# Layer-0 projection, output projection and scan: sums and transposes in two parts, transposes amid products, scan inputs in column pieces

## The reference

```
# layer 0: input projection and per-head work (gdn_sequence)
proj = h @ w_in                                   # q, k: 8 heads; v, z: 16 heads, 128 wide
qkv = silu(short_conv(qkv, conv_w))               # 4 taps along the tokens
q, k = l2norm(q), l2norm(k)                       # per token and head
...                                               # delta rule, both directions -> o_f, o_b
o = rmsnorm(o_f + flip(o_b), norm_g) * silu(z)
y = o.reshape(B, T, 2048) @ w_out                 # output projection of layer 0
# layer 1: gates and scan (rglru_sequence)
r = sigmoid(xblk @ w_r + b_r); i = sigmoid(xblk @ w_i + b_i)
log_a = -8 * r * softplus(-lam); a = exp(log_a)
b = sqrt(-expm1(2 * log_a)) * (i * xc)
h = scan of h[t] = a[t] * h[t-1] + b[t], once forwards, once backwards
```

## Time and profile before

| what | value |
|---|---|
| median of 3 runs | 4576.62 us (4575.06 to 4580.44) |
| profiled execution: its own time, and its span | 4570.06 us, 4568.1 us |
| TensorE busy | 4101.5 us (90%), 30756 matmuls |
| VectorE, ScalarE, GpSimd busy | 2332.6, 2279.5, 2017.4 us |
| mean granted clock of TensorE | 0.948 of full speed |
| costliest groups | L565 (products of the projection), three of 710 to 725 us |

### The profile page before, as it was taken

How to read it: one execution, slowest core, us unless ns; L and a number is a source line. 1 busy time by engine, 2 the same in 40 slices (tenths; PEclk the granted TensorE clock), 3 DMA queues, 4 the chain that set the end, 5 groups by cost and what they waited for, 6 DMA issues and landing times. The chain is left out here.

```text
span 4568.1 us, 83170 instructions
## 1 busy us (share of the span) xinstructions
PE 4101.5 (90%) x30756; PEld 3422.6 (75%) x30756; DVE 2332.6 (51%) x2947; ACT 2279.5 (50%) x4473; POOL 2017.4 (44%) x1524
## 2 busy tenths in 40 slices
PE   6689999999999969999999999986999599978779
PEld 2367777777777758888888888875888488856657
DVE  3234433444434446666666666655554423238853
ACT  4335555555654636666666666652111511148832
POOL 2245555555545546677777777743111412100022
PEclk8789999999999989999999999998999599988889
DMA  6245544445445456676667666654443322354245
GB/s 229 86 126 149 150 141 143 146 145 149 143 144 149 145 177 198 198 200 197 198 197 199 196 200 197 200 166 172 175 178 138 97 105 113 126 204 188 82 136 138
DMA packets 775798, 733.24 MB, mean 161 GB/s; under 512 B 111808, under 2 KB 702656, under 8 KB 758272
## 3 DMA queue, kind: packets, MB, share of 16 engines
q1 hardware_dynamic: 775456, 728.67, 51.3%
HBM read 483.12 MB, written 245.33 MB: 159 GB/s over the span
## 5 line engine op out<-in xcount | busy, mean ns | idle before, releaser
L565 PE MATMUL pj_bank<-h_hi,pj_whi 128*128 128x512 f32 (+1 forms) x1920 | 724.6, 377 | 21.0 <-POOL pj_wlo L551 20.8
L565 PE MATMUL pj_bank<-h_lo,pj_whi 128*128 128x512 f32 (+1 forms) x1920 | 711.7, 371 | 0.0
L565 PE MATMUL pj_bank<-h_hi,pj_wlo 128*128 128x512 f32 (+1 forms) x1920 | 710.0, 370 | 0.0
L751 POOL TENSOR_TENSOR pj_BD<-pj_E,pj_gi 128x512 f32<-128x512 f32 x144 | 194.6, 1352 | 650.4 <-ACT pj_E L888 650.4
L1354 ACT ACTIVATE dc_R<-dc_psE 128x256 f16<-128x256 f32 x864 | 285.0, 381 | 371.4 <-PE dc_psE L1231 371.3
L1428 DVE TENSOR_TENSOR dc_Y<-dc_psY,dc_pick 128x256 f16<-128x256 f32 x864 | 325.1, 417 | 277.7 <-PE dc_psY L1217 277.7
L565 PEld LDWEIGHTS pj_bank<-h_hi,pj_whi 128*128 128x128 f32 x1920 | 366.8, 191 | 88.9 <-POOL pj_wlo L551 21.3
L565 PEld LDWEIGHTS pj_bank<-h_lo,pj_whi 128*128 128x128 f32 x1920 | 365.9, 191 | 64.9 <-issue 5.7
L565 PEld LDWEIGHTS pj_bank<-h_hi,pj_wlo 128*128 128x128 f32 x1920 | 365.1, 190 | 62.0
L933 DVE RECIPROCAL pj_acc<-pj_acc 128x2304 f32<-128x2304 f32 x16 | 232.8, 14553 | 260.8 <-ACT pj_acc L865 260.8
L1146 POOL TENSOR_TENSOR dc_A<-dc_Lhi,dc_id 128x512 f16<-128x512 f16 x144 | 166.3, 1155 | 416.0 <-ACT dc_Lhi L1345 416.0
(11 more groups left out here) (267 smaller groups left out, 10394.3 us busy)
## 6 DMA issues: line engine op xcount, KB each, us to landing
dc_dd<-scratch_decays SPq DMA_DIRECT2D x288, 256.0 KB, 5.5
dc_tm<-scratch_tm SPq DMA_DIRECT2D x288, 192.0 KB, 2.5
pj_E<-scratch_cgrow SPq DMA_DIRECT2D x288, 128.0 KB, 3.7
scratch_decays<-pj_E SPq DMA_DIRECT2D x144, 256.0 KB, 3.8
scratch_decays<-pj_BD SPq DMA_DIRECT2D x144, 256.0 KB, 3.7
dc_fm<-scratch_fm SPq DMA_DIRECT2D x288, 128.0 KB, 3.3
dc_egr<-scratch_egrow SPq DMA_DIRECT2D x288, 128.0 KB, 3.7
scratch_o<-dc_ob SPq DMA_DIRECT2D x288, 128.0 KB, 3.1
```

Of the source, the lines that this page charges most:

```text
L565: i = pe.matmul(self.bank[blk][:, 0:n], l[b][:, k, :], r[:, k, at:at + n], start=(m == 0), stop=(m == 3 * KT - 1))
L751: pool.tensor_tensor(BD[b][:], E[b][:], gi[b][:, :, Q_BETA, :].unsqueeze(3).broadcast_to(C4), ALU.mult).then_inc(s["d_scaled"], 1)
```

## The change

**Projection of layer 0.** The sums and transposes are cut in two parts, pieces 0 to 2 and pieces 3 and 4 (`PARTS`). Part 0 stands after block 3, part 1 after block 4. The keys' transposes stand later by one block: part 0 after V0's block 4, part 1 after V1's block 0. ScalarE's reads are cut alike (`beside`). The store of the keys' transposes moves on SyncE's queue behind two `finish`.

```diff
+        PARTS = (range(3), range(3, NB))
@@ sync, stage
-                    if j == V1:
-                        store_tm(h, "trK", 0)
                     if j:
                         finish(h, j - 1, 2, last)
...
                     finish(h, j, 0, last)
+                    if j == V1:
+                        store_tm(h, "trK", 0)
@@ tensor, stage
                         pr.products(pe, h, j, blk, first)
-                        if blk != 3:
+                        if j == V0 and blk == NB - 1:
+                            turn(h, K, "trK", 0)
+                        if j == V1 and blk == 0:
+                            turn(h, K, "trK", 1)
+                        if blk < 3:
                             continue
                         if j == Q and not first:
-                            turn(h - 1, V1, "trV1")
+                            turn(h - 1, V1, "trV1", blk - 3)
                         if j == Z0:
-                            norms(h, Q)
+                            norms(h, Q, blk - 3)
                         if j == Z1:
-                            norms(h, K)
-                        if j == V0:
-                            turn(h, K, "trK")
+                            norms(h, K, blk - 3)
                         if j == V1:
-                            turn(h, V0, "trV0")
+                            turn(h, V0, "trV0", blk - 3)
@@ scalar
+                def beside(h, j, first, part):
+                    if j == Q and not first:
+                        collect(h - 1, V1, "trV1", part)
+                    if j == Z0:
+                        root(h, Q, part)
+                    if j == Z1:
+                        root(h, K, part)
+                    if j == V0 and part == 1:
+                        collect(h, K, "trK", 0)
+                    if j == V1:
+                        collect(h, V0, "trV0", part)
+
                 def stage(h, j, first):
                     decay(h, j, 0)
                     take(h, j, 0, first)
+                    if j == V1:
+                        collect(h, K, "trK", 1)
                     take(h, j, 1, first)
...
                     take(h, j, 2, first)
                     take(h, j, 3, first)
...
+                    beside(h, j, first, 0)
                     decay(h, j, 2)
                     take(h, j, 4, first)
+                    beside(h, j, first, 1)
```

```diff
-        EARLY, LATE = range(4), range(4, NV)
+        EARLY, LATE = range(9), range(9, NV)
+        BEFORE_TURN = 12
@@ tensor
+                    if is_first(i):
+                        turn(0)
                     pe.wait_ge(s["lo"], i + 1)
...
-                        row_products(pe, NV, yp[j], hi[j], lo[j], whi, wlo, w_lo).then_inc(s["y"], 1)
+                        row_products(pe, NV, yp[j], hi[j], lo[j], whi, wlo, w_lo, range(BEFORE_TURN))
+                        turn(1)
+                        row_products(pe, NV, yp[j], hi[j], lo[j], whi, wlo, w_lo, range(BEFORE_TURN, NV)).then_inc(s["y"], 1)
...
+                        if half == 0 and not last:
+                            turn(i + 1)
                     t.then_inc(s["y"], 1)
-                pipeline(pe, NCH, (0, turn), (-1, products))
+                pipeline(pe, NCH, (0, products))
@@ vector
-                pipeline(dve, NCH, (0, turned), (1, add), (0, low), (0, late), (1, norms), (1, early), (-1, residual))
+                pipeline(dve, NCH, (0, turned), (0, low), (0, late), (1, add), (1, norms), (1, early), (-1, residual))
```

```diff
+        FIRST = ((CTX, 512), (CTX + 512, 512), (CTX + 1024, 1024), (0, CTX))
...
+                def first_halves():
+                    for n, (at, w) in enumerate(FIRST):
+                        for half, name in ((xhi, "xhi"), (xlo, "xlo")):
+                            src = dram[name][0:2].rearrange("s p t -> p s t")[:, :, at:at + w]
+                            sp.dma_start(half[0][:, :, at:at + w], src).then_inc(load_first[n], 16)
...
-                halves_load(0)
+                first_halves()
...
+            @block.gpsimd
+            def _(pool):
+                for b in range(1, LB):
+                    pool.wait_ge(s["w_hi"], b)
+                    pool.wait_ge(load_w[b % 2], 64 * (b // 2 + 1))
+                    pool.tensor_copy(whi[b % 2][:], w_raw[b % 2][:]).then_inc(s["w_hi"], 1)
...
-                    if w_split_after(u):
-                        w_split(w_split_after(u))
```

More of the change, by code:

```diff
@@ L775, in _, with norms @@
             def _(pe):
-                def norms(h, j):
-                    pe.wait_ge(s["square"], nth(h, j, "qk"))
+                def norms(h, j, part):
+                    if part == 0:
+                        pe.wait_ge(s["square"], nth(h, j, "qk"))
                     base = aux_before(h, "ssQ" if j == Q else "ssK")
-                    for b, (at, n) in enumerate(BLKS):
+                    for b in PARTS[part]:
+                        at, n = BLKS[b]
                         if b >= 3:
@@ L786, in norms, with turn @@
                                   ).then_inc(s["aux"], 1)
-                def turn(h, j, use):
-                    if j == K:
+                def turn(h, j, use, part):
+                    if part == 0 and j == K:
                         pe.wait_ge(s["norm"], nth(h, j, "qk"))
-                    else:
+                    elif part == 0:
                         pe.wait_ge(s["silu"], nth(h, j, "qkv"))
                     base = aux_before(h, use)
-                    for b in range(NB):
+                    for b in PARTS[part]:
                         if b >= 3:
@@ L867, in root, with collect @@
                                        ).then_inc(s["aux_read"], 1)
-                def collect(h, j, use):
+                def collect(h, j, use, part):
                     base = aux_before(h, use)
-                    if not (isinstance(h, int) and h == 0 and j == K):
+                    if part == 0 and not (isinstance(h, int) and h == 0 and j == K):
                         act.wait_ge(s["tm_out"], 16 * nth(h, j, "kv") - 16)
-                    for b in range(NB):
+                    for b in PARTS[part]:
                         n = min(TRB, NCH - TRB * b)
@@ L904, in stage @@
                     take(h, j, 3, first)
[L905 to L914 removed]
+                    beside(h, j, first, 0)
                     decay(h, j, 2)
                     take(h, j, 4, first)
+                    beside(h, j, first, 1)
                 sweep(act, stage)
                 silu(NQ - 1, V1)
[L919 removed]
+                for part in range(2):
+                    collect(NQ - 1, V1, "trV1", part)
             @block.vector
@@ L1534, in weights_low, with row_products @@
             eng.tensor_tensor(wlo[:, k, :], raw[:, k, :], whi[:, k, :].bitcast(F32), ALU.subtract).then_inc(s_lo[own], 1)
-def row_products(pe, rows, banks, hi, lo, whi, wlo, s_lo):
-    for k in range(rows):
+def row_products(pe, rows, banks, hi, lo, whi, wlo, s_lo, some=None):
+    for k in range(rows) if some is None else some:
         pe.wait_ge(s_lo[k % 2], k // 2 + 1)
@@ L1655, in _, with turn @@
                 pe.wait_ge(s["gate_read"], 2)
-                def turn(i, j, w, first):
+                def turn(i):
                     pe.wait_ge(s["scaled"], i + 1)
@@ L1665, in products @@
                 def products(i, j, w, first):
+                    last = isinstance(i, int) and i == NCH - 1
+                    if is_first(i):
+                        turn(0)
                     pe.wait_ge(s["lo"], i + 1)
@@ L1960, in _ @@
                         for c, g, at, w in pieces(parts):
+                            if u == 0:
+                                for done, (start, width) in zip(load_first, FIRST):
+                                    if start <= at < start + width:
+                                        pe.wait_ge(done, 32)
                             m = 0
```

29 lines of the change are left out of this document (10 added, 19 removed).

## The result

The changed kernel takes **4509.98 us** (median of 4 runs, 4505.83 to 4515.37); before, beside it, 4575.84 (4 runs, 4560.26 to 4580.44). The ratio is 0.9863, with a 95% interval of 0.9846 to 0.9879. Forecast were 4517, in a range of 4472 to 4556. The profiled execution took 4508.69 us, with a span of 4506.9.

The account below looks back on a forecast made before the run. TensorE was taken to bound the projection, its small waits costing idle time and clock. From 4570.06, −32 (projection), −20 (output projection) and −8 (scan) gave 4510, plus 6.6 to the median: 4517 us, range 4472 to 4556.

Parts of the forecast that it names:

- What goes: Projection: TensorE's waits for ScalarE's reads of sums and transposes, 43.6 + 32.8 = 76.4 us, can all go.
- The clock: Projection: half-speed stretches after TensorE's waits cost 28 us of full-speed work, 3.5 us a head, which goes with the waits.
- so 1.7 us more: Projection, V1: a new 5 us wait brings back 3.4 us at half rate, costing 1.7 us a head.
- The keys' store: Projection: the later store of the keys' transposes makes TensorE wait in V1, at least 1.8 us, 5 with queue delay.
- The norms' latency: Projection: keys are normalised 25 us after Z1's block 4, later against the products, while V0 with second sums takes 26.5.
- The transposes, a block later, just get them: Projection: the keys' transposes get the norms in time, with margin 1.5 us and cost 0 to 1.
- Rival B: Projection: the decay chain with two buffers becomes the bound and heads keep their length; 4549 us, chance 0.15.
- Rival A: Projection: the keys' store lands in time and the queue is not late; 80 to 104 us go, 4457 us, chance 0.17.
- C: Projection: SyncE's queue is late in K, V0 and V1; at 20 us of new waits a head 4604 us, chance 0.05.
- D: Output projection: its start gains nothing, as weight splitting in nine early rows pushes everything back; 4537 us, chance 0.06.
- Output projection: Its start: first products at about 3100.5, chunk 1's at 3127 to 3133 instead of 3151; −20 us, bounds −23 and −8.
- scan: Three weight copies leave ScalarE for GpSimd, 5.7 us, and an earlier start gives 3 us; −8 us, bounds −12 and −2.

Follow-up runs that it names:

- e9: The changed kernel with TensorE's eight projection heads written out instead of looped, the keys' store where the change has it: 4490.3 us, ratio 0.9814.
- e4: The changed kernel with the store of the keys' transposes moved up in SyncE's queue, ahead of the end of item V1.0: 4504.8 us, ratio 0.9873.
- e5: The changed kernel with the keys' store moved up and decay items cut to one of GpSimd's three products (timing only): 4485.4 us, ratio 0.9806.
- e6: The changed kernel with decay items cut to one of GpSimd's three products, keys' store not moved up (timing only): 4494.4 us, ratio 0.9829.
- e7: The changed kernel with TensorE's eight projection heads written out and the keys' store moved up: 4483.6 us, ratio 0.9806.

## Why the prediction was right, point by point

**What goes: right.** The waits of sums and transposes were to go wholly. Of 43.6 us on the sums 6.5 are left, which the prediction had (1 us a head of squares, 8 in all), and of the transposes' waits 24 of 26 us stand in V1, where it said.

**The clock: the gain was over-estimated.** 28 us were to go and 1.7 a head to come back, 14 net. Busy time at half speed fell by 17.2 us, which is 8.6 net. The step that was off is "so 1.7 us more": behind the wait in V1 the clock is low for 10.2 us and not for 3.4, with 4.7 to 7.2 us of work in it (in five of six heads; 6.8 us with 3.4 of work in the last), where a second gap follows 1.5 us behind the first. In e9, without the second gap, the stretch behind V1's wait is 3.4 us long in four heads and 6.8 in one, and in one there is none. That the clock falls when TensorE rests, the part of the rule of the Trainium skill (TensorE: Matmul & The Clock Gate, Part 1) used there, fits these rows too.

**The keys' store: right in place and size.** The working counts from V0's end, and takes for it 917.64, when ScalarE took the last block at once, as it had waited for it. In the changed kernel ScalarE is 3.1 us late there, so the count must start on TensorE, at 894.27. Forecast: issued at + 21, with 3 us for the queue + 24; landed at + 32.2; TensorE at its wait at + 28.6; a wait of 5. In the head shown the store is issued at + 25.7 and has landed at + 32.2, TensorE stands there from + 28.4, and the wait is 4.49; the six middle heads' mean is 4.0. Two errors offset each other: the queue was 1.7 us later than the 3 allowed, and the landing took 6.5 us in place of 8.0. That TensorE went on 0.65 us behind the landing, and not 1.2, makes up the rest.

**The norms' latency: right.** "The transposes, a block later, just get them" came with a margin of 1.0 us in the head shown (1.5 forecast) and one wait of 0.9 us in another, and heads are 173 us apart (927.12 - 754.17 = 173.0), which was the forecast.

**What was missing: the loop's head.** The sum had no term for it: 15.6 us in five waits by "issue" and one of 2.7, 18 us, and with the clock 16 to 23 by e9. It was missing because the row of before is this, over the whole phase:

```profile
PE pj_bank L565 <- issue: 0.2, 1, 0.2
```

Before, block 4 of V1, 24 long products, stood between the last wait and the branch. Now six transposes, which wait, are the last thing ahead of it. The written-out kernels show that the gap is the loop's. What uncovers it is argued: e4, where TensorE doesn't wait in V1 but the six transposes are still last, has 2.0 us on average in place of 3.1, so the short work ahead of the branch seems to be the larger part and the wait the smaller. No kernel was tried with the loop kept and long products last. The Trainium skill (Runtime: NRT & Kernel Launch, Instruction fetch mechanics) says that a taken branch out of the prefetched stretch waits for a fetch; the 3 us agree in kind, and no run here shows a fetch.

This term and the other errors cancel: the forecast put 56 us of new waits (8 x 7) against 76.4 removed, 51.1 came, made of 25 on `pj_tm` (24 of them in V1), 18 at the loop's head and 7 or so on the sums. Waits came out 5 us better than forecast and the clock 6 us worse. The 7 us by which the projection beat the sum are thus mostly the 6 us of busy time that neither waits nor clock give, and the 3 us that the forecast took off for the first and the last head; in size they are like the scatter. The total was right, in part by luck: only half of the new waits are the ones named.

**The rivals.** Rival B, the items as the bound, did not come, since the head didn't keep its length. But e5 and e6 show that the items, or what their products hold up, are on the path beside TensorE's own gaps: shorter ones gave 12 to 24 us. Rival A (the store in time) would have been worth 0 to 5 us, not 60, by e4. Rivals C and D did not come: new waits were 6.4 us a head against C's 16.6, and the phase that D doubted gave 18.1 us.

**Output projection and scan: right.** Products from 3099.6 (forecast 3100.5) and chunk 1's from 3132.2 (3127 to 3133); -18.1 for -20. In the scan -9.8 (-10.9 over all traces) for -8: the copies 6.7 for 5.7 and the start 4.2 for 3.

## What to carry to other kernels

A wait just removed should be asked what it covered: here the wait moved to within six transposes of a loop's end, and the branch, free before, cost 3 us a turn. Write the loop out on the engine that is the bound (16 to 23 us here), or, not tried here, keep long work that waits for nothing between the last wait and the loop's end. And a wait should be priced by what arrives next and not by its length: in e4 24 us of waits in V1 went and 0 to 5 us were won, as others grew in their place, while the gaps at the loop's head came back whole once they were gone.

## What the runs showed of the hardware

- A loop's end on TensorE: 0.2 us in one of six turns and nothing in the others behind 24 long products (before), 1.2 to 3.0 us behind six transposes that didn't wait (e4), 2.7 to 3.7 us behind six that waited for 3 to 5 us (after), 0 when written out (e7, e9).
- Two rests of 4.5 and 3 us with 1.5 us of work between them were covered by one stretch at the 1.2 GHz level of 10.2 us (five heads of six; 6.8 in the last). Single rests of up to 5.2 us went with 3.4 us where the clock fell at all, and with 6.8 once each in before and in e9.
- How long SyncE takes to issue a store depends on the transfers ahead: an item's first store took 2.6 to 3.3 us in six heads when it was issued 0.8 us behind the 1152 KB store of the keys' transposes (e4), and 0.4 to 0.6 when issued 2.7 to 3.3 us behind it (after). So the transfer ahead holds up the queue itself, and not only the landing. In e4:

```profile
914.34 0.40 SPq L665 DMA_DIRECT2D scratch_tm<-pj_tm  x1
915.17 2.59 SPq L689 DMA_DIRECT2D scratch_decays<-pj_E  x1
```

In the changed kernel, behind the store issued at 920.00:

```profile
923.27 0.40 SPq L689 DMA_DIRECT2D scratch_decays<-pj_E  x1
```
